# Six places for raw weights instead of three, in memory shared between tiles

## What is computed

```python
# first block, i = 0, 1
x = x + 0.5 * swiglu(rmsnorm(x, g1), w_gate, w_up, w_down)      # width 2816
h = rmsnorm(x, mix_norm[i])
o = gla_attention(...) if i == 0 else mla_attention(...)        # mixer over the tokens
o_mem = memory_cross_attention(q_mem, rmsnorm(mem), w_kv, ...)  # 4 heads over 256 memory rows
x = x + concat([o, o_mem]) @ w_out[i]
x = x + 0.5 * swiglu(rmsnorm(x, g2), w_gate, w_up, w_down)
# second block, i = 0, 1: grouped attention of 12 heads, plus memory attention of 4
x = x + rms_norm(concat([tok, mo]) @ w_o[i], g_mix_post[i])
x = x + rms_norm((silu(h @ gate) * (h @ up)) @ w_down[i], g_ffn_post[i])
```

## Time and profile before

| | |
|---|---|
| median of 3 runs | 1731.2 us (1731.12 to 1731.95) |
| the profiled execution's own time | 1737.8 us |
| its span, first to last instruction | 1736.0 us |
| mean granted TensorE clock | 0.983 of full |
| PE busy | 1669.3 us, 96% |
| DVE busy | 1218.3 us, 70% |
| ACT busy | 944.4 us, 54% |
| read from memory | 285 MB, mean 165 GB/s |

### The profile page before, as it was taken

One profiled execution on the slowest core, in us unless ns is written; L12 is line 12 of the kernel. 1 busy time (PEld: TensorE's weight loads), 2 busy tenths in 40 slices (PEclk: granted clock), 3 DMA queues, 4 the chain that ended last, 5 costly groups with the idle time before them and its releaser, 6 DMA issues.

```text
span 1736.0 us, 28058 instructions
## 1 busy us (share of the span) xinstructions
PE 1669.3 (96%) x10124; PEld 1472.3 (85%) x10124; DVE 1218.3 (70%) x1680; ACT 944.4 (54%) x1518; POOL 87.1 (5%) x96
## 2 busy tenths in 40 slices
PE   9999999899999999998899999997999999899998
PEld 8999987799999899987689899885888878588887
DVE  6876786467666786676656776757677667767765
ACT  5655563555555565555655654556565554746553
POOL 0100011000000100002400100000000001000000
PEclk9999999999999999999999999998999999899999
DMA  7666545256655466555324565441465554136563
GB/s 235 205 211 187 163 159 157 85 178 198 203 184 181 146 200 199 181 167 161 122 79 158 185 207 186 154 158 51 142 225 188 191 160 133 49 118 224 192 189 101
DMA packets 79328, 287.00 MB, mean 165 GB/s; under 512 B 8848, under 2 KB 9232, under 8 KB 79008
## 3 DMA queue, kind: packets, MB, share of 16 engines
q1 hardware_dynamic: 78192, 282.17, 50.2%
q0 software_dynamic: 608, 3.15, 0.5%
q10 hardware_dynamic: 464, 0.82, 0.2%
HBM read 285.05 MB, written 1.05 MB: 165 GB/s over the span
## 4 chain that ended last, share of the span: by engine, by line
PE 80%; DVE 9%; ACT 4%; DMA 4%; issue 2%; POOL 0%; SPq 0%; ACTq 0%; DVEq 0%; POOLq 0%
PE ps L2025 25%; PE ps L2029 13%; PE ps L1938 7%; PE ps L1989 6%; PE ps L1990 6%; PE ps L1991 6%; DMA raw<-units 4%; PE ps L2004 3%; PE ps L2005 3%; PE ps L2006 3%; DVE wlo L1218 2%; ACT whi L796 1%; PE ps L2399 1%; DVE acts L1252 1%; PE ps L2461 1%
## 5 line engine op out<-in xcount | busy, mean ns | idle before, releaser
L1382 DVE TENSOR_TENSOR wlo<-raw,whi 128x1024 fp32r<-128x1024 f32 x380 | 463.8, 1223 | 124.8 <-ACT whi L926 123.5
L2025 PE MATMUL ps<-acts,whi 128*128 128x512 f32 x2016 | 505.9, 393 | 4.6 <-DVE prob L1389 4.0
L926 ACT ACTIVATE whi<-raw 128x1024 fp32r<-128x1024 f32 x380 | 398.2, 1051 | 97.4 <-PE ps L2029 65.2
L2025 PEld LDWEIGHTS ps<-acts,whi 128*128 128x128 f32 x2016 | 365.3, 189 | 72.7 <-DVE prob L1389 4.4
L2029 PEld LDWEIGHTS ps<-acts,wlo 128*128 128x128 f32 x2016 | 275.0, 190 | 19.7
L2029 PE MATMUL ps<-acts,wlo 128*128 128x256 f32 x2016 | 281.1, 282 | 0.0
L1218 DVE TENSOR_TENSOR wlo<-raw,whi 128x1024 fp32r<-128x1024 f32 x154 | 188.4, 1240 | 110.7 <-ACT whi L796 109.8
L1938 PE MATMUL ps<-whi,acts 128*128 128x512 f32 (+3 forms) x772 | 219.5, 376 | 11.3 <-ACT arena L877 6.0
L796 ACT ACTIVATE whi<-raw 128x1024 fp32r<-128x1024 f32 x154 | 159.9, 1056 | 128.7 <-DMA raw<-units 95.5
L1989 PE MATMUL ps<-hid_hi,wlo 128*128 128x256 f32 x704 | 199.3, 283 | 0.0
L1990 PE MATMUL ps<-hid_hi,whi 128*128 128x256 f32 x704 | 199.3, 283 | 0.0
(11 more groups left out here) (239 smaller groups left out, 2079.7 us busy)
## 6 DMA issues: line engine op xcount, KB each, us to landing
raw<-units SPq DMA_DIRECT2D x534, 512.0 KB, 4.2
arena<-mem_in POOLq DMA_DIRECT2D x2, 1024.0 KB, 8.1
x<-x_in SPq DMA_DIRECT2D x4, 256.0 KB, 5.0
arena<-mem_in POOLq DMA_DIRECT2D x4, 256.0 KB, 4.9
out<-x SPq DMA_DIRECT2D x4, 256.0 KB, 2.1
const<-const_in ACTq DMA_DIRECT2D x1, 560.0 KB, 3.4
row<-row_in ACTq DMA_DIRECT2D x1, 134.0 KB, 3.4
gain<-gain_in ACTq DMA_DIRECT2D x1, 76.5 KB, 4.1
```

What stands on the lines that cost most here:

```text
L926: nc.scalar.activation(whi[:, u % RING, :], raw[:, u % RAW, :], ACT.Copy).then_inc(hi_ready, 1)
L1382: V.tensor_tensor(wlo[:, u % RING, :], raw[:, u % RAW, :], whi[:, u % RING, :].bitcast(F32), ALU.subtract).then_inc(lo_ready, 1)
L2025: T.matmul(ps[:, bank, :], whi[:, slot, w], acts[:, k].rearrange("p e s -> p (e s)"), start=k == 0, stop=False)
```

## The change

The number of raw places goes from 3 to 6, as many as `whi` and `wlo` have. The 12 KB more per partition come from shared homes. `sil` and `hid` are halves of one tile `hidden`, which is also `qmT`. `probT` lies in the first half of `rows`, and `square_q` in `vm`. `alpha` and `lowT` lie in `vm` too. SP now issues the first six loads without waiting, with the identity's load between the third and the fourth, as before; after that the load of unit u waits for the lowering of unit u-6. No other wait, instruction or order differs.

```diff
-RAW, RING, LEAD = 3, 6, 4
+RAW, RING, LEAD = 6, 6, 4
...
-        sil = sb("sil", [P, 2, S])
-        hid = sb("hid", [P, 2, S])
+        hidden = sb("hidden", [P, 4, S])
+        sil, hid = hidden[:, 0:2, :], hidden[:, 2:4, :]
...
-        probT = sb("probT", [P, 2, TT, S])
+        probT = rows[:, 0, :].rearrange("p (k t s) -> p k t s", k=2, t=TT)
...
-        qmT = sb("qmT", [P, 4, S])
+        qmT = hidden[:]
...
-        alpha = sb("alpha", [GRANK, 512])
-        lowT = sb("lowT", [GRANK, S])
+        alpha, lowT = vm[0:GRANK, 0, :], vm[0:GRANK, 1, 0:S]
...
-        square_q = probT[:].rearrange("p k t s -> p (k t s)").rearrange("p (t n) -> p t n", t=TT)
+        square_q = vm
...
-            for u in range(1, RAW):
+            for u in range(1, RING):
+                if u == 3:
+                    sp.dma_start(const[:, 0:P], const_in[:, 0:P]).then_inc(ident_landed, 16)
                 load(u, u)
-            sp.dma_start(const[:, 0:P], const_in[:, 0:P]).then_inc(ident_landed, 16)
-            for u in range(RAW, RING):
-                sp.wait_ge(lo_ready, u - RAW + 1)
-                load(u, u % RAW)
```

## The result

The changed kernel takes 1717.7 us in the median of 4 runs (1715.2 to 1718.6), the kernel before 1731.6 in the same sitting. The ratio is 0.992, 95% interval [0.9902, 0.9938]. Forecast was 1715.7, range 1709 to 1724. The profiled execution of the changed kernel took 1718.5 for a span of 1716.6 us, with a mean granted clock of 0.991 (before: 1737.8, 1736.0 and 0.983).

The account below looks back on a forecast made before the run. PE was taken as the bound, busy 1669.3 of 1736.0 us, with idle stretches fed by late raw loads. Gains 1.4 + 4.2 + 1.6 + 2.0 + 5.6 + 0.7 = 15.5 us off 1731.2 gave 1715.7, range 1709 to 1724.

Parts of the forecast that it names:

- loads slow each other: Rival: engines serve all loads in turn, the first land late (3.6 us), nothing returns elsewhere; 1734.8 us, chance 0.03.
- the prediction's rule against it: HBM access slows at high load, so landing goes from 4.2 to 6 us, still under the lead of 7.
- Start: Kernel start: DVE's wait for the sixth split and PE's pause at 22.84 shrink, 1.4 us; lower end a 2.2 loss.
- Gated linear mixer: PE's pause of 2.87 us until 278.54: 2.7 back, plus 1.5 of lost clock, together 4.2 us.
- The two blocks: Third and fourth feed-forward blocks: ACT's load waits before the memory rows' squares vanish, 1.6 and 2.0 us.
- Latent mixer: Several pauses in a row, followed by the late engine: first scores 5.6 us earlier, bounds 4.3 and 8.5.
- (c): Latent mixer: PE's pause of 1.10 at 830.62, for a lowering, stays or grows; DVE stays 4.3 us ahead.
- (b): Latent mixer: DVE reaches its evacuations 4.3 us earlier; PE's pause of 2.31 at 813.15 shrinks to about 0.4.
- (e): Latent mixer: DVE waits for POOL's power, whose chain is only 4.3 us ahead; scores come 4.3 + 1.3 earlier.
- Last mixer: DVE's evacuation at 1453.14, late by a load-bound lowering, comes earlier: 0.7 us, between 0 and 1.0.
- PE's lead counts in full: Rival, latent mixer: POOL's operations could pair otherwise with DVE's; total 1711.5 us, chance 0.12.
- The next late engine is closer: Rival: a pause closed in one place opens in the next; blocks and half the mixers return, 1722.6 us, chance 0.20.

Follow-up runs that it names:

- experiment 1: Changed kernel with six places and shared homes, but each load waits for the lowering of the unit three back, as before: 1729.9 us, ratio 1.0007.
- experiment 2: Changed kernel with loads issued four units ahead in place of six: 1717.2 us, ratio 0.993.
- experiment 6: Kernel before, with the latent mixer's two DVE lowerings moved ahead of its wait for POOL's power: 1731.5 us, ratio 0.9998.
- Experiment 7: Changed kernel with two of POOL's four products of the latent query rotation left out, so queries are wrong: 1717.1 us in one run.
- experiment 10: Changed kernel with only the first six loads early; from the seventh unit on, loads wait for the unit three back: 1733.1 us, ratio 1.0014.
- distance 3: Loads wait for the lowering of the unit three back; the table's three such profiles are the kernel before, its repetition (1731.6 us) and experiment 1.
- experiment 12: Changed kernel, latent mixer: one DVE lowering ahead of POOL's power, three behind the takes of the turned queries: 1716.8 us, ratio 0.9929.
- experiment 11: Changed kernel with two latent-mixer lowerings moved behind the takes, plus 92 idle matmuls ahead of PE's waits: 1716.4 us, ratio 0.9924.

## Why the prediction was right, and where it was not

**The mechanism.** Right. ACT's waits for raw went from 127 us to 0.2, DMA left the chain, and experiment 1 shows that nothing else of the change moves the time by more than its interval of 0.2%. PE's idle time was to fall to about 53 us; it fell to 58.4, and to 55.1 in the second trace. The estimate of a lead of 7 us against 4.2 was ample; experiment 2 shows that one unit more than before would do. The rival "loads slow each other" is right of the start and wrong of the rest. There the three extra loads landed 7.0, 7.8 and 8.5 us after their issue, where the kernel before, issuing them later, has 3.3, 3.2 and 4.3. But units 1 and 2, issued before them, landed at 9.20 and 10.52 us in place of 9.17 and 10.44, so the order of issue was the order of service, as assumed, and the lower end of -2.2 fell. Behind the start loads go out at PE's pace, whatever the number of places: four or more are hardly ever in flight, the median stays at 4.2, and a landing time with six in flight throughout was not measured. The 6 us that the prediction's rule against it arrived at were passed by those three loads and by no typical one.

**Start** (1.4): 1.1. DVE no longer waits for ACT there. The first stamp comes at 21.2 to 21.4. It came at 22.8 in the execution that I read, but at 22.0 and 22.3 in the two others of its kind: the pause of 1.51 in the earlier trace rows was a large draw, with 0.68 and 0.96 in the other two.

**Gated linear mixer** (4.2): 4.0. Of the 2.7 for the pause 2.4 to 2.5 came (2.87, 2.85, 2.88 against 0.42). The 1.5 for the clock is a price that the pause has in most executions, not in all: with the same pause of 2.85, the repetition of the kernel before kept a clock of 1.00 in the window from 276 to 286, where the other two have 0.83, and none of the traces without the pause has a lower clock there.

**The two blocks** (1.6 and 2.0): 1.7 and 2.0, with no smaller waits returned on top.

**Latent mixer** (5.6): 3.4, the step that failed. Up to (c) it went as written, a little better at the end: POOL starts its rotation 4.8 us earlier from the mixer's start, where I had 4.3. The pause of (b) shrank to 0.82, not to 0.4. The pause of (c) did stay and grow. In (e) I took POOL's chain as a fixed length. From the start of the rotation to the end of the power it takes 18.2 us in the kernel before and 20.0 in the changed one. The rows of the kernel before, POOL and then DVE:

```profile
839.54 2.20 POOL L758 TENSOR_TENSOR arena<-prob 128x512 f32<-128x512 f32 x1
841.70 1.28 POOL L759 TENSOR_TENSOR arena<-prob 128x512 f32<-128x512 f32 x1
843.06 0.21 POOL L660 TENSOR_SCALAR means<-sums 128x16 f32<-128x16 f32 x1
```

```profile
839.39 1.21 DVE L1218 TENSOR_TENSOR wlo<-raw,whi 128x1024 fp32r<-128x1024 f32 x1
840.53 1.27 DVE L1301 TENSOR_SCALAR arena<-ps,rstd 128x1024 f32<-128x1024 f32 x1
844.29 2.36 DVE L1218 TENSOR_TENSOR wlo<-raw,whi 128x1024 fp32r<-128x1024 f32 x2 [2.49 <-ACT whi L796]
```

There DVE waited 2.49 us for ACT, which waited for a load, and so its two lowerings came after POOL's product and mean. With the loads on time they moved into them. The wait that was removed had kept two engines apart, and not even reliably. In the repetition of the kernel before that wait was 1.02 us, so the two lowerings met the mean and the power, and POOL's chain took 19.7 us there already:

```profile
840.31 2.40 DVE L1218 TENSOR_TENSOR wlo<-raw,whi 128x1024 fp32r<-128x1024 f32 x2 [1.02 <-ACT whi L796]
```

```profile
840.57 1.07 POOL L660 TENSOR_SCALAR means<-sums 128x16 f32<-128x16 f32 x1
841.72 3.75 POOL L663 TENSOR_TENSOR rstd<-means,minus_half 128x16 f32<-128x16 f32 x1
```

So the account of the first pair of traces is 4.8 for DVE, less 1.8 for POOL's longer chain, plus 1.6 that follow POOL's end faster (the forecast's 1.3): 4.6, against 5.6. A further 2.5 us of that pair went behind the scores: from them to ffn21 it took 82.1 us before and 84.6 after, with pauses of 2.51 and 3.25 in a row and this window of the changed kernel:

```profile
840.00:850.00 10.00, 4.24 (x17) 3.16 (x16) 6.02 (x10) 1.97 (x2) 1.58 (x2) 0.79 0.31 105
```

This is not a draw. The stretch from the scores to ffn21 goes with POOL's chain in every trace. Where the chain took 15.6 to 18.2 us (the kernel before, experiments 1, 6, 7 and 10), it takes 82.1 us, and the scores begin at full clock. Where the chain took 19.1 us or more, it takes 83.5 to 84.6, and in all of these without idle matmuls the clock falls around the first scores. What PE did before differs as follows: its pauses at the turns and at the scores are 1.2 to 1.4 us in the first group and 2.3 to 5.8 in the second. The first 4 us of the scores in the kernel before and in its repetition, the one trace at distance 3 with a long chain, show it:

```profile
858.10:862.10 4.00, 3.67 (x16) 2.91 (x16) 2.74 (x8) 1.95 (x7) 0.00 (x0) 1.00 0.07 29
```

```profile
855.60:859.60 4.00, 4.00 (x12) 3.27 (x13) 1.71 (x4) 1.60 (x5) 0.00 (x0) 0.62 0.31 107
```

Experiment 7 changed nothing but POOL's chain and moved the kernel from the second group to the first. So a late POOL costs twice, before the scores and behind them, and the sum had no term for the second. Since the repetition is among the three distance-3 traces (83.7), the mean loss is 1.4, not 2.5: 4.8 earlier at the scores less 1.4 is the 3.4 of the table.

The row that would have warned me was there: the same kind of operation on the same shape took 2.20 us beside a lowering (L758) and 1.28 alone (L759).

**Last mixer** (0.7): the pause fell from 1.02 to 0.74, but the stage scatters by 5 us, so its share is open. **The last two rows** of the table had a forecast of 0.7 together and show 3.4. Executions of the same timing differ there by as much or more. The sum of 15.6 thus agrees with the forecast better than its terms do, and that is luck: 2.2 too much in the latent mixer, 2.7 too little in stages that draw. By the medians the gain is 13.8, less than forecast by 1.7, about the latent mixer's miss; with runs that scatter by 3 us that agreement is no proof.

**The rivals.** "PE's lead counts in full" fell with POOL's chain, which held it. It had named the thing that happened, POOL's operations pairing otherwise with DVE's, and took it for a gain. "The next late engine is closer" had the right mechanism in one mixer (DVE's lowering at 819.81, POOL's chain at 843.10) and not in the rest.

## What to carry to other kernels

When a wait is taken away, list not only what comes earlier but what it will now run beside; a chain whose length is read from the old trace keeps it only if its neighbours stay. For a buffer's depth, compute the lead that covers issue to landing and stop there: here a lead of four units gave all that six gave. A change of a few microseconds is seen at its stage's stamps in several traces, since the runs of one kernel in one sitting differ by up to 10 us in total.

## What the runs showed of the hardware

**VectorE and GpSimd hold each other up.** A lowering (a tensor_tensor with both inputs in SBUF) and a GpSimd operation on SBUF don't share, they take turns. In the changed kernel the rows at 830.9 can be read as a queue: one lowering (1.2 us), then the product (1.2), then the second lowering (1.1), then the mean; the rows give the sums, the split is an estimate. The pair of lowerings takes 3.43 us in place of 2.36, the product 2.35 in place of 1.28, the mean 1.07 in place of 0.21, and taking one lowering out (experiment 12) restored the mean to 0.21. The Trainium skill, "SBUF — State Buffer", section "SBUF: two separate sides", describes this as an exclusive lock on a shared port pair, held for a whole instruction by a GpSimd operation or, against a GpSimd operation that reads SBUF, by a VectorE operation with two SBUF inputs. The rows agree with it in each of these numbers.

**The granted clock differs between executions of the same work.** The first grouped mixer took 125.8, 128.3 or 130.3 us, at distance 3 (experiments 1 and 6 and the kernel before) as with early loads (the changed kernel, experiments 2 and 7). In the latent mixer it does not draw: there the clock at the scores goes with the length of the pauses before them. Idle matmuls bought the clock back (loss from 12.8 to 6.0 us in experiment 11) and gave nothing in the end.

**Loads in flight together take turns.** At the start of the changed kernel, with the three extra loads, the DMA engines move 406 GB/s from 4 to 12 us where they moved 346, the extra loads land 7.0 to 8.5 us after issue, and those issued first land within 0.1 us of where they did. At the mean rate behind that, the median is 4.0 to 4.2 us whether a load may be issued three, four or six units ahead.
